# The T1 product ahead of the T4 product in the first five steps of a ConvFFN's up-projection loop

## The reference, cut to what matters

```python
def conv_ffn(xn, buf, w_up, cw, cb, w_down):
    up = xn @ w_up                                  # 1024 -> 2 * 2816
    upc, new_buf = causal_dwconv(up, buf, cw, cb)   # width 3
    val, gate = jnp.split(upc, 2, axis=-1)
    return (jax.nn.gelu(gate) * val) @ w_down, new_buf
```

## Time and profile before

| | us |
|---|---|
| median of 3 runs | 1045.46 (1044.52 to 1046.51) |
| the profiled execution | 1043.88 |
| its span in the trace | 1042.1 |
| PE busy | 1013.1 (97%) |
| DVE busy | 743.4 (71%) |
| ACT busy | 520.4 (50%) |
| POOL busy | 420.6 (40%) |

### The profile page before, as it was taken

One profiled execution on the slowest core, in us unless ns is written; L12 is line 12 of the kernel. 1 busy time (PEld: TensorE's weight loads), 2 busy tenths in 40 slices (PEclk: granted clock), 3 DMA queues, 4 the chain that ended last, 5 costly groups with the idle time before them and its releaser, 6 DMA issues.

```text
span 1042.1 us, 20026 instructions
## 1 busy us (share of the span) xinstructions
PE 1013.1 (97%) x7688; PEld 988.9 (95%) x7688; DVE 743.4 (71%) x1270; ACT 520.4 (50%) x936; POOL 420.6 (40%) x286
## 2 busy tenths in 40 slices
PE   8999999999999999999999989899999999999985
PEld 7899999999999999999999988899999999999985
DVE  6788457956746567385635799998888787878654
ACT  7576787314343444442522456655555545555553
POOL 4333334333222223233133446666454545454430
PEclk9999999999999999999999998999999999999997
DMA  8633432478487686783652422323232323232137
GB/s 199 191 85 94 106 79 76 104 190 220 91 241 200 141 257 146 191 228 93 207 187 80 125 61 82 102 62 112 72 112 71 113 71 112 72 107 76 36 93 217
DMA packets 263268, 132.95 MB, mean 128 GB/s; under 512 B 82720, under 2 KB 257045, under 8 KB 262920
## 3 DMA queue, kind: packets, MB, share of 16 engines
q1 hardware_dynamic: 262966, 131.63, 46.1%
q10 hardware_dynamic: 210, 0.07, 0.0%
HBM read 104.17 MB, written 25.29 MB: 124 GB/s over the span
## 4 chain that ended last, share of the span: by engine, by line
PE 80%; DVE 8%; issue 5%; DMA 2%; POOL 2%; ACT 1%; SPq 0%; DVEq 0%; POOLq 0%; ACTq 0%
PE ring L2747 40%; PE bank L3138 11%; PE ring L3152 10%; PE ring L3138 9%; PE bank L2989 2%; PE bank L2793 1%; POOL wlo L1226 1%; DVE bank L1880 1%; DMA d_stage<-in_w_down 1%; POOL f_lo L1269 1%; PE bank L2972 1%; PE bank L3069 1%; PE bank L2900 1%; PE bank L3057 1%; DMA y<-out_rows 1%
## 5 line engine op out<-in xcount | busy, mean ns | idle before, releaser
L1226 POOL TENSOR_TENSOR wlo<-stage,whi 128x1024 fp32r<-128x1024 f32 x78 | 197.6, 2534 | 397.3 <-ACT whi L1282 397.3
L2747 PE MATMUL ring<-x_split,whi 128*128 128x322 f32 (+2 forms) x1952 | 347.5, 300 | 0.0
L2747 PEld LDWEIGHTS ring<-x_split,whi 128*128 128x128 f32 x1952 | 294.5, 189 | 8.9 <-issue 8.1
L2747 PE MATMUL ring<-x_split,wlo 128*128 128x256 f32 (+1 forms) x976 | 210.4, 297 | 0.0
L2747 PEld LDWEIGHTS ring<-x_split,wlo 128*128 128x128 f32 x976 | 164.6, 189 | 0.0
L1282 ACT ACTIVATE whi<-stage 128x1024 fp32r<-128x1024 f32 x79 | 83.4, 1055 | 93.7 <-PE ring L2747 77.5
L1269 POOL TENSOR_TENSOR f_lo<-f_stage,f_hi 128x512 fp32r<-128x512 f32 x78 | 103.9, 1348 | 57.5 <-ACT f_hi L1663 57.5
L1269 POOL TENSOR_TENSOR f_lo<-d_stage,f_hi 128x512 fp32r<-128x512 f32 (+1 forms) x48 | 57.8, 1204 | 119.2 <-ACT f_hi L1663 119.1
L3138 PE MATMUL bank<-fx_T,f_hi 128*128 128x290 f32 x264 | 79.3, 301 | 4.4 <-DVE ring L2609 4.2
L1663 ACT ACTIVATE f_hi<-f_stage 128x512 fp32r<-128x512 f32 x112 | 69.0, 628 | 27.8 <-PE bank L3138 25.9
L3138 PE MATMUL bank<-fx_T,f_lo 128*128 128x290 f32 x264 | 78.3, 297 | 0.0
(11 more groups left out here) (430 smaller groups left out, 2359.1 us busy)
## 6 DMA issues: line engine op xcount, KB each, us to landing
stage<-in_w_in SPq DMA_DIRECT2D x56, 512.0 KB, 4.2
f_stage<-in_w_up SPq DMA_DIRECT2D x44, 512.0 KB, 5.3
d_stage<-in_w_down SPq DMA_DIRECT2D x40, 256.0 KB, 2.8
stage<-in_w_branch_a SPq DMA_DIRECT2D x8, 512.0 KB, 3.6
c_sample<-in_state_mlstm_C SPq DMA_DIRECT2D x16, 256.0 KB, 6.5
out_s_mlstm_C<-c_sample SPq DMA_DIRECT2D x16, 256.0 KB, 2.4
stage<-in_w_branch_b SPq DMA_DIRECT2D x8, 512.0 KB, 3.8
stage<-in_w_out SPq DMA_DIRECT2D x8, 512.0 KB, 3.8
```

The lines of the kernel that those rows point to most:

```text
L1226: pool.tensor_tensor(spaced(wlo[:, slot]), packed(stage[:, slot, 0:n]), spaced(whi[:, slot]).bitcast(F32), ALU.subtract).then_inc(w_lo, 1)
L2747: last = pe.matmul(of(z, t0 or -2, t1), w[:, kk * WS:kk * WS + P], x_, start=kk == 0 and m == 0, stop=kk == kn - 1 and m == 2)
```

## The change

For steps i below LAG = 5 the table, ACT's program and PE's program put T1(i) ahead of T4(i-1). From step 5 on nothing is moved.

```diff
@@ weight_order
         if d:
             yield "D", *d
-        if i:
+        if i >= LAG:
             yield "T4", i - 1
         yield "T1", i
+        if 0 < i < LAG:
+            yield "T4", i - 1
         yield "B21", i
@@ ACT's program of a step
                 if d:
                     ahead("D", *d)
-                if i:
+                if i >= LAG:
                     ahead("T4", i - 1)
                 part_five(i)
+                if i < LAG:
+                    ahead("T1", i)
+                    if i:
+                        ahead("T4", i - 1)
                 if i:
                     first_tap(i - 1, 0)
                 part_two(i)
-                ahead("T1", i)
+                if i >= LAG:
+                    ahead("T1", i)
                 ahead("B21", i)
@@ PE's program of a step
-                if i:
+                if i >= LAG:
                     pe.wait_ge(sum_added, ADDED["C22", i - 1])
                     up_product("T4", i - 1, False)
                 if i:
@@
                 up_product("T1", i, True)
+                if 0 < i < LAG:
+                    pe.wait_ge(sum_added, ADDED["C22", i - 1])
+                    up_product("T4", i - 1, False)
                 if i:
                     pe.wait_ge(sum_scaled, SCALED["C11", i - 1])
```

## The result

| | before | after |
|---|---|---|
| median of 6 runs each, us | 1046.38 (1044.52 to 1048.45) | 1049.68 (1047.98 to 1051.77) |
| the profiled execution, us | 1043.88 | 1047.98 |
| ratio to before | | 1.0038, 95% interval 1.0024 to 1.0052 |

What follows compares the result with a forecast made beforehand. DVE bounds steps 1 to 4, PE's idle time being its lead. Terms of -0.15 us (PE) and +3.25 us (DVE, on C22(4)) gave +3.1 us; on the median of before, 1045.46, that is 1048.6 us, range 1045.0 to 1051.5.

Steps and rivals of the forecast that it cites:

- PE's 4.4 us of idle time are DVE's lead, and DVE is the bound: Steps 1 to 4 and start of 5: PE idles 4.4 us waiting for DVE's C22 additions; DVE busy 50.65 of 54 us.
- T4(4): PE, step 5, unmoved product: held by C22(4)'s addition, it would start at 697.2 against 694.21, with a stall of some 0.6 us.
- the lower bound: DVE, steps 1 to 4: taps win every turn, paying only ACT's lateness, 0.9 us a step; sum 50.4, PE gains 2.9 and 0.15.
- Nothing behind 694 gives back or takes up: PE from 694 to 990 us is never idle, so what it gains or loses by 694 arrives at the end unchanged.
- Term one, -0.15 us: PE at T4(4), DVE's times held: starts 0.25 us sooner, loses 0.1 us to a restart; -0.15 us.
- The 4.1 us of recoverable stalls: PE before T4, steps 1 to 4: T1 fills at most min(1.6, stall) per step, 0.3 + 1.1 + 1.6 + 1.1 us.
- Steps 2 and 3 of DVE, 13.75 us each: From one C22 addition to the next: POOL's low parts delay the first tap and come between both taps; 13.75 us each.
- Step 1, 14.25 us: DVE's first step: 13.75 us, plus a block of L2457 by B11(2)'s low part, 0.36 before and 0.15 more; 14.25 us.
- Step 4, 14.8 us: DVE's step 4: L2470 blocked, ending at 7.33, taps granted at 8.57 and 10.4, ending at 11.05; 14.8 us.
- Free of blocking, that step is 11.7 us: DVE, step 3 before: 12.38 less 0.57 (L2470) and 0.14 (block of L2457) gives 11.7 us.
- the case of no change: Rival, chance 0.22: blocks of L2470 and L2479 traded for blocks of the taps, DVE's sum within 2 us of 53.3; 1045.3 us.
- the much slower one: Rival, chance 0.10: POOL keeps its turns, or L2479 is caught again in each step; 1050.8 to 1053.7 us.

Runs made afterwards that it cites:

- before with short low parts: Kernel before, with POOL's low parts of T1, T4 and B21 of pairs 2 to 5 made for 2 of 128 columns only; ratio 0.9972.
- the two with four holds: Kernel before, one low part on POOL held until DVE's value taps are done in each of steps 1 to 4; PE's new order 0.9968, old order 0.9987.

## Why the prediction was right

It said 1048.6 us in a range of 1045.0 to 1051.5 and 0.70 for slower. Measured were 1049.68; of the 1.1 us between them 0.9 are the median of before, 1046.38 over six runs where the prediction had 1045.46 from three. Step by step:

- **PE's 4.4 us of idle time are DVE's lead, and DVE is the bound** until T4(4): right. T4(4) waited for C22(4)'s addition, or followed it within 0.3 us, in every kernel but three: before with short low parts (DVE's sum 49.75) and the two with four holds (50.6). There PE took over. So the lower bound would not have been reached in full: it has PE gain 3.05 us at a sum of 50.4, and at 50.55 T4(4) came 2.55 sooner.
- **Nothing behind 694 gives back or takes up**: right up to C22(21) (3.77 against 3.86 us). Behind it, in the last steps, 0.8 us came back (DVE's last addition starts at 1032.68 against 1028.36, 4.32 us later where C22(21) was 5.13 later). PE's timeline has them in three waits behind C22(21), in the last products: 0.77, 2.54 and 0.44 us before (992.02, 998.78, 1008.24), 0.62, 2.03 and 0.28 after.
- **Term one, -0.15 us**: the run with TensorE's order alone gave +1.0 us (-0.3 to 2.4), with DVE's sum 0.7 us longer. What failed is "with DVE's times held": PE's new order brings ACT's copy of T2 and, behind it, POOL's low part sooner into the taps of steps 1 and 3 (+1.06 and +0.99 us), and takes 0.67 off each of steps 2 and 4. That the two nearly cancel, so that term one came out near, is luck. That the lead is spent at T4(4) was right. The 4.1 us of recoverable stalls do not follow from the rows either (0.94, 1.6 and 0.83 make 3.4, and step 1 a few tenths); nothing in the sum hangs on them.
- **Steps 2 and 3 of DVE, 13.75 us each**: 13.77 and 13.78. The sum for T2 free, the tap ready at 7.2 behind C22 (656.16 to 663.35), POOL between the taps: each as said.
- **Step 1, 14.25 us**: 14.75. The term that was mis-sized is the block by B11(2)'s low part, put at 0.15 us (0 to 0.4) above the 0.36 before. Its lateness was right: the load is issued 2.44 us ahead of C22(0) in place of 3.69, 1.25 us later. But the low part then missed the sum for T3 and met that for T1 at its very start:

```profile
645.18 0.68 DVE L2464 TENSOR_TENSOR f_stage<-f_stage 128x512 f32<-128x512 f32 x1
645.79 1.78 DVE L2465 TENSOR_TENSOR f_stage<-f_stage 128x512 f32<-128x512 f32 x1
```

```profile
644.70 0.63 ACT L1665 ACTIVATE f_hi<-f_stage 128x512 fp32r<-128x512 f32 x1 [1.17 <-DMA f_stage<-in_w_up]
```

```profile
645.41 1.60 POOL L1271 TENSOR_TENSOR f_lo<-f_stage,f_hi 128x512 fp32r<-128x512 f32 x1 [1.00 <-ACT f_hi L1665]
```

  That is 1.78 - 0.68 = 1.10 us of block, 0.6 more than the 0.51 in the sum. A lateness was priced where a meeting should have been looked for.
- **Step 4, 14.8 us**: 15.02. The taps end 10.89 us behind C22's addition, 0.16 sooner than worked out, but 4.13 us follow them, not 3.77. The rows of step 4 before had the same 4.13 (686.69 + 2.62 to 693.44), with DVE idle for 0.46 us behind the taps; the prediction took the 3.77 of step 3.
- **"Free of blocking, that step is 11.7 us"**: wrong, and without effect on the sum. With short low parts before still takes 12.26, because the taps cannot start before ACT's tap ends, 6.8 us behind C22 (672.54 + 0.89 against 666.67). So "before, the tap was out of DVE's way" failed too: it ended 0.16 us ahead of DVE's taps, and the block of the sum for T2 before (0.57) cost 0.12 to 0.14 us (12.38 against 12.26 for the step, 6.92 against 6.78 for the start of the taps). The traded block that the case of no change counted on was worth little for this reason.
- **The waits on PE**: T1 1.0 (1 to 1.6 said), T4 0.41 to 0.44 (0.6), T3 0.27 (0.5), T4(4) 0.40 (0.6). The 1.10 us in D(0, 0) at 697.79, for the low part of the last product, were not foreseen; they lie ahead of T4(4)'s wait and cost nothing beside it.
- **The exclusion of POOL and DVE**, and the rule of the Trainium skill (SBUF — State Buffer, "Who interferes with whom") that spoke against the change: this case's runs agree, since the taps fall from 2.81 to 1.71 us when POOL's work is cut short. That POOL gets the turn between the two taps came from the rows and held wherever POOL had a low part queued at the taps.
- **The price against the median**: 3.1 us forecast, 3.8 in the trace, 4.0 (2.5 to 5.4) in the runs. The rivals of faster and of nothing fell because the blocks were traded upwards, and the much slower one is near what ScalarE's and GpSimd's part gave alone, in the trace by taps of 3.9 us, but with the clock's fall in it, which the prediction did not have. In the case of nothing, the two prices are exchanged: it is L2479 that was blocked for 1.1 us and L2470 for 0.57 to 0.7.

## What to carry to other kernels

Before giving an idle slot of the busiest engine a better order, ask which engine's chain sets the wait; here TensorE's order was worth 1.2 to 2 us once VectorE's chain was short, and nothing measurable in the kernel before. An order written for one engine carries the others' lists with it: move them apart and price each, above all where two engines exclude each other, as VectorE and GpSimd do in these sums and taps. A wait put on the engine with slack can keep it out of the critical one's way, but it pays only where the postponed work lands behind instructions that it does not disturb; check where the backlog goes. And a profiled execution that lies well above the median of its kernel needs a look at the granted clock, stretch by stretch, before its waits are explained.

## What was not expected of the hardware

- A block costs about the time that POOL still had to run, 0.12 or 0.13 us less in three cases. DVE's sum of 0.68 us that POOL caught at 672.42 in before, 0.69 us ahead of POOL's end, took 1.25 and ended 0.56 us after that end (673.11 to 673.67); L2479 at 680.20 took 1.80 with 1.25 us of POOL left. In the change the sum that met a low part at its start took 1.78, 1.1 more. POOL's low parts in turn went from 1.27 to 1.83 us each where taps lay between them.
- Two VectorE instructions in a row from the same list do not keep the turn. With work queued on GpSimd, it came between the two taps each time (2.6 to 2.8 us for the pair, 3.6 to 3.9 where a low part also stood ahead of the first), and holding it by a semaphore kept it out (1.69 to 1.71).
- Stalls of the same length left TensorE's granted clock alone in one kernel and not in another. In step 3 of before PE stood idle for 2.45 us, and the clock stayed at 1.00 (667.19 to 678.00). With the order of ScalarE and GpSimd alone it stood idle for 2.44 us in step 3, and the clock was 0.50 from about 674 to 677.
